# Rotary step of a two-block transformer kernel: cosine and sine products on GpSimd, sine rows added by its DMAs

## The reference, cut to what matters

```python
def partial_rope(x, cos, sin):
    half = ROPE_DIM // 2
    x1, x2, xp = x[..., :half], x[..., half:ROPE_DIM], x[..., ROPE_DIM:]
    return jnp.concatenate([x1 * c - x2 * s, x1 * s + x2 * c, xp], axis=-1)
...
q_rope = partial_rope(qn, cos, sin)
k_sl = partial_rope(rmsnorm(heads(ksl, KVH), nsa_knorm_g[i, 1]), cos, sin)
k_wn = partial_rope(rmsnorm(heads(kwn, KVH), nsa_knorm_g[i, 2]), cos, sin)
```

## Time and profile before

| | |
|---|---|
| median of 3 runs | 989.2 us (lowest 988.89, highest 989.45) |
| the profiled execution's own time | 991.16 us |
| its span, first to last instruction | 989.5 us |
| PE busy | 968.3 us (98%) |
| DVE busy | 754.5 us (76%) |
| ACT busy | 617.7 us (62%) |
| POOL busy | 6.9 us (1%) |
| granted TensorE clock | 1.00 of full speed |

### The profile page before, as it was taken

One profiled execution on the slowest core, in us unless ns is written; L12 is line 12 of the kernel. 1 busy time (PEld: TensorE's weight loads), 2 busy tenths in 40 slices (PEclk: granted clock), 3 DMA queues, 4 the chain that ended last, 5 costly groups with the idle time before them and its releaser, 6 DMA issues.

```text
span 989.5 us, 18815 instructions
## 1 busy us (share of the span) xinstructions
PE 968.3 (98%) x7642; PEld 880.5 (89%) x7642; DVE 754.5 (76%) x1132; ACT 617.7 (62%) x918; POOL 6.9 (1%) x17
## 2 busy tenths in 40 slices
PE   6999999999999999999999999999999999999997
PEld 6998888998978889989998999999988988888886
DVE  7968676787676786797778776868977698768675
ACT  5745785676437775778467655556666576555564
POOL 2000000000000000000000000000000000000000
PEclk9999999999999999999999999999999999999999
DMA  9665513365637131835655656556473456655541
GB/s 304 200 167 171 171 60 112 123 218 172 174 118 229 44 124 53 272 117 182 202 170 174 210 172 202 178 187 203 120 235 99 148 168 198 191 195 184 178 161 43
DMA packets 143357, 164.00 MB, mean 166 GB/s; under 512 B 6302, under 2 KB 129832, under 8 KB 143288
## 3 DMA queue, kind: packets, MB, share of 16 engines
q1 hardware_dynamic: 142408, 161.97, 51.1%
q10 hardware_dynamic: 464, 0.93, 0.3%
q0 software_dynamic: 416, 0.12, 0.1%
HBM read 161.95 MB, written 1.05 MB: 165 GB/s over the span
## 4 chain that ended last, share of the span: by engine, by line
PE 79%; DVE 10%; ACT 4%; DMA 3%; issue 2%; SPq 0%; DVEq 0%; ACTq 0%
PE ps L483 16%; PE ps L484 16%; PE ps L485 16%; PE ps L1263 14%; PE ps L1261 7%; DVE panels_low L2005 3%; DMA panels<-in_w_in 2%; ACT panels_high L1377 2%; DVE squares L1968 1%; PE ps L501 1%; PE ps L688 1%; DVE input_parts L1964 1%; PE ps L713 1%; DMA panels<-in_w_pg 1%; PE ps L784 1%
## 5 line engine op out<-in xcount | busy, mean ns | idle before, releaser
L2005 DVE TENSOR_TENSOR panels_low<-panels,panels_high 128x2048 fp32r<-128x2048 f32 (+1 forms) x145 | 327.5, 2262 | 80.0 <-ACT panels_high L1377 79.8
L1377 ACT CAST panels_high<-panels 128x2048 fp32r<-128x2048 f32 (+1 forms) x145 | 273.1, 1886 | 101.4 <-PE ps L485 64.0
L483 PE MATMUL ps<-input_parts,panels_low 128*128 128x256 f32 x832 | 241.6, 290 | 2.2 <-DVE panels_low L2005 1.5
L484 PE MATMUL ps<-input_parts,panels_high 128*128 128x256 f32 x832 | 235.2, 283 | 0.0
L485 PE MATMUL ps<-input_parts,panels_high 128*128 128x256 f32 x832 | 235.1, 283 | 0.0
L1263 PE MATMUL ps<-input_parts,panels_high 128*128 128x512 f32 x608 | 214.0, 395 | 0.0
L1261 PE MATMUL ps<-input_parts,panels_low 128*128 128x256 f32 x608 | 170.6, 281 | 0.7 <-DVE panels_low L2005 0.7
L483 PEld LDWEIGHTS ps<-input_parts,panels_low 128*128 128x128 f32 x832 | 159.1, 191 | 7.4 <-issue 3.9
L484 PEld LDWEIGHTS ps<-input_parts,panels_high 128*128 128x128 f32 x832 | 159.2, 191 | 0.7 <-issue 0.5
L485 PEld LDWEIGHTS ps<-input_parts,panels_high 128*128 128x128 f32 x832 | 159.2, 191 | 0.0
L1263 PEld LDWEIGHTS ps<-input_parts,panels_high 128*128 128x128 f32 x608 | 114.1, 188 | 26.4
(11 more groups left out here) (342 smaller groups left out, 1620.8 us busy)
## 6 DMA issues: line engine op xcount, KB each, us to landing
panels<-in_ffn_up SPq DMA_DIRECT2D x44, 1024.0 KB, 5.1
panels<-in_w_in SPq DMA_DIRECT2D x29, 1024.0 KB, 5.5
panels<-in_ffn_down SPq DMA_DIRECT2D x22, 1024.0 KB, 4.8
panels<-in_mix_w_in SPq DMA_DIRECT2D x20, 1024.0 KB, 5.5
panels<-in_w_out SPq DMA_DIRECT2D x8, 1024.0 KB, 5.0
panels<-in_w_pg SPq DMA_DIRECT2D x8, 1024.0 KB, 5.1
panels<-in_mix_w_out SPq DMA_DIRECT2D x8, 1024.0 KB, 5.2
panels<-in_w_in SPq DMA_DIRECT2D x6, 512.0 KB, 5.7
```

Of the source, the lines that this page charges most:

```text
L483: pe.matmul(dst, w[1], x[0], start=start, stop=False if not kw else True, **kw)
L484: pe.matmul(dst, w[0], x[1], start=False, stop=False if not kw else True, **kw)
L1377: nc.scalar.copy(high_slots[slot][:, 0:size], raw[n % SLOTS][:, 0:size]).then_inc(high_ready, 1)
L2005: V.tensor_tensor(low_slots[slot][:, 0:size], raw[n % SLOTS][:, 0:size], high_slots[slot][:, 0:size].bitcast(F32), ALU.subtract).then_inc( ...
```

## The change

The turning leaves PE. After the norm (L2316 and L2327 before), GpSimd waits for DVE, multiplies the normed q by the cosine table into q_rope and by a sine table with its signs in it into the second half of the tile squares, and does the same for k inside k_rope_terms. Then GpSimd issues four DMAs for q and four for k. Each takes 8 rows of the sine part, which are the other half of a head's 16 rows, and adds them in SBUF to the cosine part. The copies into k_padded read SBUF now and stand later in ACT's list. PE waits before its first mask product for the adds of q and for k_padded.

```diff
-    rot = np.zeros((P, P))
...
-        sin[h:h + 8] = np.sin(ang.astype(np.float32))
+        sin[h:h + 8] = np.sin(ang.astype(np.float32)) * (-1 if h % 64 else 1)
...
-                pe.wait_ge(rope_ready, l + 1)
-                for j in range(2):
-                    begin(f"qr{j}_{l}", 1 + j)
-                    pe.matmul(ps[1 + j][:, :], ident, UW[:, j * 512:(j + 1) * 512], start=True, stop=False)
-                    done(f"qr{j}_{l}", pe.matmul(ps[1 + j][:, :], const("rot"),
-                                                 UW[:, 1024 + j * 512:1024 + (j + 1) * 512],
-                                                 start=False, stop=True))
-                    todo(("copy", f"qr{j}"))
                 some(2)
                 gate_chunk()
-                pe.wait_ge(k_rope_ready, l + 1)
-                begin(f"kr_{l}", 4)
-                pe.matmul(ps[4][:, :], ident, UK[:, 0:512], start=True, stop=False)
-                done(f"kr_{l}", pe.matmul(ps[4][:, :], const("rot"), UK[:, 512:1024], start=False, stop=True))
-                todo(("k_pad",))
...
                 todo(("o_square",))
+                todo(("k_pad",))
...
-                drained(pe, f"qr1_{l}")
-                drained(pe, f"kr_{l}")
+                pe.wait_ge(q_turned, 64 * (l + 1))
+                pe.wait_ge(kz_ready, l + 1)
...
-                        name = f"kr_{l}"
-                        full(act, name)
-                        src = v3(bank(name), 2)
+                        act.wait_ge(k_turned, 64 * (l + 1))
+                        src = UK[:, 0:512].rearrange("p (k t) -> p k t", k=2)
...
-                        act.wait_ge(rope_ready, l + 1)
+                        act.wait_ge(kz_ready, l + 1)
...
-                    parts_out = (parts_out or step == "hidden_parts") and (step, *arg) != ("copy", "qr1")
+                    parts_out = (parts_out or step == "hidden_parts") and step != "hidden"
...
-                        qn4 = v3(QN, 4)
-                        for i, tab in enumerate(("cos", "sin")):
-                            ins = V.tensor_tensor(UW[:, i * 1024:(i + 1) * 1024].rearrange("p (j t) -> p j t", j=4),
-                                                  qn4, const(tab).unsqueeze(1).to_broadcast([P, 4, T]), ALU.mult)
-                        ins.then_inc(rope_ready, 1)
+                        V.scalar_tensor_tensor(QN[:, :], QN[:, :], GQ[:, l:l + 1], HZ[:, :],
+                                               ALU.mult, ALU.mult).then_inc(q_normed, 1)
...
+            def turned(terms, cosine, table, heads):
+                return nc.gpsimd.tensor_tensor(cosine.rearrange("p (j t) -> p j t", j=heads),
+                                               terms.rearrange("p (j t) -> p j t", j=heads),
+                                               const(table).unsqueeze(1).to_broadcast([P, heads, T]), ALU.mult)
+
+            half_rows = [(h + a, h + 8 - a) for h in (0, 64) for a in (0, 8)]
+
+            pool.wait_ge(const_landed, 16)
+            for l in range(DEPTH):
+                pool.wait_ge(q_normed, l + 1)
+                turned(QN[:, :], QR[:, :], "cos", 4)
+                turned(QN[:, :], UW[:, 1024:2048], "sin", 4).then_inc(rope_ready, 1)
+                pool.wait_ge(rope_ready, l + 1)
+                for src, dst in half_rows:
+                    pool.dma_start(QR[dst:dst + 8, :], UW[src:src + 8, 1024:2048], accum_op=ALU.add).then_inc(q_turned, 16)
+                pool.wait_ge(k_normed, l + 1)
+                turned(KN[:, :], UK[:, 0:512], "cos", 2)
+                turned(KN[:, :], UK[:, 512:1024], "sin", 2).then_inc(k_rope_ready, 1)
+                pool.wait_ge(k_rope_ready, l + 1)
+                for src, dst in half_rows:
+                    pool.dma_start(UK[dst:dst + 8, 0:512], UK[src:src + 8, 512:1024], accum_op=ALU.add).then_inc(k_turned, 16)
```

More of the change, by code:

```diff
@@ L372, in build @@
         kc_rinv_ready, o_rinv_ready = sem("cmp_k_rinv_ready"), sem("hg_o_rinv_ready")
+        q_normed, k_normed = sem("q_normed"), sem("k_normed")
         rope_ready, k_rope_ready = sem("q_rope_terms_ready"), sem("k_rope_terms_ready")
+        q_turned, k_turned = sem("q_sine_terms_added"), sem("k_sine_terms_added")
+        kz_ready = sem("k_padded_ready")
         blocks_ready = sem("cmp_blocks_ready")
@@ L1563, in _ @@
                 log_exp()
-                dest = {"nq0": QN[:, 0:512], "nq1": QN[:, 512:1024], "qr0": QR[:, 0:512], "qr1": QR[:, 512:1024],
-                        "ct": PCT[:, :], "hgo0": SG[:, 0:512], "hgo1": SG[:, 512:1024],
+                dest = {"nq0": QN[:, 0:512], "nq1": QN[:, 512:1024], "ct": PCT[:, :], "hgo0": SG[:, 0:512], "hgo1": SG[:, 512:1024],
                         "hz0": HZ[:, 0:512], "hz1": HZ[:, 512:1024], "nz0": NZ[:, 0:512], "nz1": NZ[:, 512:1024]}
@@ L1623, in _ @@
                             ins = nc.scalar.copy(kz[64:128, :, 1, g, :], s)
-                        ins.then_inc(free(name), 1)
+                        ins.then_inc(kz_ready, 1)
                     elif step == "spread":
@@ L2315, in _ @@
                         dve.wait_ge(q_rinv_ready, l + 1)
-                        link(V.scalar_tensor_tensor(QN[:, :], QN[:, :], GQ[:, l:l + 1], HZ[:, :],
-                                                    ALU.mult, ALU.mult))
-                        qn4 = v3(QN, 4)
-                        for i, tab in enumerate(("cos", "sin")):
-                            ins = V.tensor_tensor(UW[:, i * 1024:(i + 1) * 1024].rearrange("p (j t) -> p j t", j=4),
-                                                  qn4, const(tab).unsqueeze(1).to_broadcast([P, 4, T]), ALU.mult)
-                        ins.then_inc(rope_ready, 1)
+                        V.scalar_tensor_tensor(QN[:, :], QN[:, :], GQ[:, l:l + 1], HZ[:, :],
+                                               ALU.mult, ALU.mult).then_inc(q_normed, 1)
                     elif kind == "k_norm":
@@ L2326, in _ @@
                             s = slice(j * T, (j + 1) * T)
-                            step(V.scalar_tensor_tensor(KN[:, s], KN[:, s], vec("nsa_knorm_g", 3 * l + 1 + j),
-                                                        UK[:, 512 + j * T:512 + (j + 1) * T], ALU.mult, ALU.mult))
-                        settle()
-                        for i, tab in enumerate(("cos", "sin")):
-                            ins = V.tensor_tensor(UK[:, i * 512:(i + 1) * 512].rearrange("p (j t) -> p j t", j=2),
-                                                  v3(KN, 2), const(tab).unsqueeze(1).to_broadcast([P, 2, T]),
-                                                  ALU.mult)
-                        ins.then_inc(k_rope_ready, 1)
+                            ins = V.scalar_tensor_tensor(KN[:, s], KN[:, s], vec("nsa_knorm_g", 3 * l + 1 + j),
+                                                         UK[:, 512 + j * T:512 + (j + 1) * T], ALU.mult, ALU.mult)
+                        ins.then_inc(k_normed, 1)
                     elif kind == "hidden":
```

## The result

The changed kernel takes **996.34 us** (median of 4 runs, 995.96 to 996.99) against 989.33 us (4 runs of the kernel before on the same chip): a ratio of **1.0072**, 95% interval 1.0055 to 1.0089. It is slower by 7.0 us. The forecast of 991.4 us had the side right and about a third of the size, and the time lies 0.8 us above the stated range.

The account below looks back on a forecast made before the run. DVE, a little ahead of a nearly full PE, was taken to decide the stretch; PE's 10.3 us and DVE's 7 us were given back as waiting, +2.2 us in all: 989.2 to 991.4 us, range 981.5 to 995.5.

Parts of the forecast that it names:

- the unknown cost that the prediction named: DVE's two-operand SBUF work beside GpSimd's products: one waits while the other's instruction runs, or they don't notice each other.
- the walk: Layer 0 timed with engines waiting in order of arrival: hgo1's split ready at 102.35, +1.1 us per layer.
- GpSimd issues q's adds to 95.6, then k's cosine product 95.9 to 97.15: GpSimd beside level six: four issues cost 2.05 us; k's cosine product starts as level six's second pair ends, 95.9.
- the chain of `hid` ... reads PSUM or one tensor and passes: DVE after level six: these rows (95.45 to 96.66 before) are not held by GpSimd and pass by 97.1.
- The rival of the kept turn: GpSimd holds through two back-to-back products; level six's second pair ends at 98.5; +5.6 us per layer, 994.8 us; chance 0.22.
- the sum without hindrance: Engines don't notice each other: 3.75 us gained per layer at hgo1, -7.5 us in all, 981.7 us; chance 0.18.
- From 101.25 on the chain stays with PE up to the masks, so I let a shift at this point go through to the end: PE from hgo1's start to the masks: the 3.75 us per layer gained at hgo1 counted in full, 7.5 us.
- The eight row transfers ... cost nothing I can see: The DMA adds of q and k, 192 KB per layer, were given no cost.
- (1): DVE rows of level six or seven with waits or lengths far above 0.42 us while POOL is busy.
- (2): POOL's 128x1024 product at 2.0 to 2.5 us.
- (3): PE idle ahead of the first product of hgo1, released by DVE's split.
- (4): No wait of PE at the first mask product and none of ACT at the copies of k.

Follow-up runs that it names:

- the two fast kernels: Changed kernel with GpSimd's products and adds started after level seven's inputs, k first: 985.12 us; changed kernel with products late on DVE, k's adds issued first: 982.23 us.
- the fills: Changed kernel with GpSimd fills in layer 0 and one-operand copies in layer 1 in place of the four products: 986.66 us (one run).

## Why the prediction was right and wrong

**Right: what bounds, and what the hindrance does.** DVE decided this stretch, PE's 10.3 us could not be had, and the unknown cost that the prediction named is the one that decided. DVE's two-operand work and GpSimd's products take turns, a whole instruction at a time, and in order of arrival where products stand back to back. The rule of the Trainium skill told in the prediction ("SBUF — State Buffer", "Who interferes with whom") holds for these, with 2.1 us on the norm of k and 1.5 us on a 128x8 multiply beside it. That the one that starts second is blocked does not fit the row of 3.40.

**Right: the walk, up to level six's second pair.** It had k's norm ending at 91.3 (91.08), the sine product at 93.5 (93.28) and the first pair at 94.4 (93.97). The product of 128x1024 was taken as 2.2 us and took 2.5, which did not matter, as it started 0.4 us earlier.

**Wrong: "GpSimd issues q's adds to 95.6, then k's cosine product 95.9 to 97.15", and the second pair that "ends at 95.9".** This is the step that failed, with two of its terms: the price of the issues and the wait. Four issues were taken as 2.05 us, from the 0.51 of the earlier trace rows. They take 3.27 us, to 96.85. Their rows start 0.52 us apart, but each is longer than the one before, so that they end 0.8 apart (the first and the last of the four):

```profile
93.58 0.84 POOL L2746 DMA_DIRECT2D q_rope<-squares  x1 [0.30 <-POOL squares L2733]
95.15 1.70 POOL L2746 DMA_DIRECT2D q_rope<-squares  x1
```

The product itself was sized right: its row of 2.46 us begins under the last issues, and it ends 1.28 us behind them, at 98.13 instead of 97.15. The wait is the second term. In the walk level six's pair passes ahead of the product. By the rows it does come first (the product's row begins at 95.67), and it is held all the same. From the chain that ended last, changed kernel:

```profile
95.12 3.33 DVE forget_key L2263
```

The pair ends at 98.45, 2.55 us later than in the walk: 1.0 of it from the longer issuing, and about 1.5 because a row that the order of arrival would have let pass was held. Why it was held stays open; the kernel with the adds behind the products shows that it goes away with the issues in front. The split of hgo1 is ready at 104.92 instead of 102.35, which is the same 2.57.

That this kernel comes out at the walk's numbers (split from 100.15 to 102.42, walk 100.05 to 102.35; 992.15 us, forecast 991.4) is luck in part. Its level seven begins its second half at 96.98 instead of the walk's 95.9, DVE's multiplies of level seven then wait for nothing where the walk has them wait until 98.4, and PE reaches hgo1 only at 103.57.

**Wrong, though it cost nothing by itself: "the chain of `hid` ... reads PSUM or one tensor and passes".** Its TENSOR_SCALAR waited for k's sine product, 1.25 us instead of 0.18. The walk had booked the same wait one step later, at level seven's multiplies.

**The rival of the kept turn gave 994.8 us, the nearest number, for the wrong reason.** It had the second pair ending at 98.5 (98.45), but two kernels show DVE getting its turn between products that stand back to back. It had a chance of 0.22, the forecast 0.38. Its number stood for any mechanism that held DVE through k's first product for 2.5 us more.

**Wrong: the sum without hindrance, -7.5 us.** With no products at all it is -3.5. The step is "From 101.25 on the chain stays with PE up to the masks, so I let a shift at this point go through to the end". Of 3.6 us at hgo1 1.4 arrive at the masks of layer 0; the rest is lost to a panel that lands late. In layer 1 3.9 us arrive; what lies between the 5.3 us of both layers and the median's 3.5 no row here places. **"The eight row transfers ... cost nothing I can see"** probably fails with it. In that kernel the adds are issued from 88.7, into the transfer of the panels (DMA share 1.0 to 1.1 from 90 on), and ACT's second cast starts at 99.57. In the two fast kernels, whose adds come after 100, it starts at 96.31 and 96.73. It is the earliest adds that go with the late panel: issued from 90.32 (the fills) the cast starts at 97.44, and issued from 90.96 (products on DVE in the old place) at 96.20, though these too run beside the panels. That is a comparison of rows, not a test of its own. In the changed kernel it starts at 96.08, so the loss is not part of the 7 us.

**Named in the prediction, and no term of the result: the granted clock.** It fell as feared, but in the changed kernel the split was later anyway: layer 0 shows it with PE's pause filled, layer 1 by PE's idle 0.84 us before hgo1.

**Points of "what would show it".** (1) came true in two rows of level six (1.69 and 3.40), and two others were held with them. (2): 2.51 and 2.54, just above 2.0 to 2.5. (3) came true in another way: PE went idle one step earlier, at level seven, and its list at half clock then filled the time up to the split. (4) came true: no wait at the first mask product, and none of ACT at the copies of k.

## What to carry to other kernels

Work moved to an idle GpSimd is not free for VectorE: with two operands in SBUF on both sides, each instruction costs the other engine up to its own length, and with DMA issues in front of it more (3.0 us on one multiply). Ask what VectorE has to deliver in those microseconds, and put the work where it is owed nothing: the same instructions gave 996.3 us in one place and 985.1 in another. Then look at what one engine's list puts ahead of what; the order of eight small transfers was worth 10.6 us, and their place between two products about 4. And before counting on time taken from a nearly full engine, check that what feeds it is early: with DVE's list as it was, 10.3 us less on TensorE gave 0.9995.

## What the runs showed of the hardware

- Issuing an add of a few rows from GpSimd keeps that engine longer than issuing a small load: four took 3.27 us, eight 6.47 (products on DVE in the old place), so 0.8 us each against 0.51 for the loads at the start. The rows start 0.52 apart and reach over the start of the next instruction, whose row is longer by it. Of the 2.46 and 2.50 us of a 128x512 product behind them 1.28 and 1.32 lie behind the last issue's end; of the 1.71 of a 128x512 fill, 0.53.
- DVE's row of 3.33 us (95.12 to 98.45) was held from 0.55 us before that product's row starts. Three other rows were held where only issues had a row at their start, or ended before the product (0.65 and 1.26 with the adds between k's products, 0.60 with the fills). Each had a product or a fill behind the issues. With nothing behind them (products on DVE in the old place, no products) DVE's rows keep 0.17 and 0.19 beside the issues. What holds them is left open.
- GpSimd's fills do not hold two-operand work on DVE, and its one-operand copies do (norm of k 0.88, 0.88 beside fills, 1.66 beside copies, 3.02 beside products). In none of the rows read here was a copy from PSUM on DVE held.
- After a pause of PE of 2.85 us its granted clock was 0.50 for about 10 us (94 to 104), with a second pause of 3.35 us in between and PE at work without a gap from 98.5 on.
